# Gate products of a recurrent layer moved to VectorE, and another order of work in a spatial gating layer

## The chip, the cores and the metric

The kernel runs on one core of a Trainium2 chip. The metric is the device time of one execution in microseconds (us). The core has five engines that run their own instruction streams in order and meet at semaphores: TensorE (PE in the profile, its weight loads PEld), VectorE (DVE), ScalarE (ACT), GpSimd (POOL) and SyncE (SP, which issues the loads of the weights).

## What is computed

Two blocks on 512 tokens of width 1024. The first (a recurrent mixer, a sparse attention, a convolution and an MLP) is not touched. The second has a chunked spatial gating layer and a recurrent layer:

```python
def chunked_sgu_mixer(h, w_in, ln_w, ln_b, w_s, b_s, w_out):
    z = h @ w_in
    u, v, g = jnp.split(z, 3, axis=-1)                 # 2048 wide each
    u = jax.nn.gelu(u)
    v = layer_norm(jax.nn.gelu(v), ln_w, ln_b)
    s = jnp.einsum('gts,bnsgc->bntgc', w_causal, v) + b_s.T[None, None, :, :, None]
    y = u * s.reshape(B, S, A_WIDTH) * jax.nn.silu(g)
    return y @ w_out

def rglru_mixer(h, ...):
    xb, g = jnp.split(h @ w_in, 2, axis=-1)            # 1536 wide each, 12 heads of 128
    xc = conv_b + sum(conv_w[k] * shifted(xb, k))      # 4 taps
    r = sigmoid(gate_a(xc));  i = sigmoid(gate_x(xc))  # one 128x128 product per head
    a = exp(-RG_C * r * softplus(-lam))
    hseq = scan(a, sqrt(1 - a * a) * (i * xc))
    y = hseq * jax.nn.silu(g)
    return y @ w_out
```

## The kernel before

**Weights.** Every weight matrix is cut into units of 128 x 1024 numbers. A unit is loaded into one of 4 slots of `raw` (`RING = 4`), ScalarE writes its rounded part `w_hi` (`hi_unit`, L358), VectorE the rest `w_lo` (`lo_unit`, L370), three units ahead of their use (`LEAD = 3`). TensorE makes each product from three matmuls, hi by hi, hi by lo and lo by hi (`three`, L386 to L388); one unit is 24 matmuls of 512 columns. The order on every engine is written by hand, with counting semaphores; a Python `for` is unrolled, a `Fori` is a loop on the chip.

**Value rows (`v`).** Four groups `g`, each of four units (`v_unit`) and four blocks of 128 tokens `t`. When a group is done, ScalarE copies a block out of its bank (L1482, `vt`), squares it into one of two buffers `e0` (L1485), VectorE makes the argument of the tanh (L2075, L2077), ScalarE the tanh (L1487), VectorE the product (L2079) and the statistics (L2081, `v_stat`). Block `t` uses buffer `t % 2`. After the last group come the mean and variance, the root on ScalarE and its reciprocal on VectorE (L2084 to L2087).

**Gating loop.** Two halves of eight chunks, two chunks (`cc` 0 and 1) per turn of a `Fori`. A chunk is a `u` unit, a `g` unit and the spatial product `mix` (L1032), which reads the normalised values `vh` of that chunk. VectorE makes `vh` (L2095, four instructions, two buffers) at the head of the chunk, then two `lo_unit`, the gelu, the gate, and at the end `h_lo` (L2126); ScalarE makes squares, tanh, sigmoid and `h_hi`; GpSimd one product (L2335). Chunk `c` uses banks 4 to 6 or 0 to 2, so TensorE starts chunk `c` when `h_ready` says that VectorE has finished chunk `c - 2`. After eight chunks, `residual` multiplies their outputs by eight units of the output weights; its first unit takes the chunks in order, the last (`k = 7`) last.

**Recurrent loop.** Two heads per turn, six turns, the first unrolled. Per turn TensorE does units `project(0..3)` (banks 0, 1, 4, 5: `x` and `g` of the two heads) and `gates(0)`, `gates(1)` (L1056, L1057). ScalarE (`turn`, L1556 on) does: unit, `read_x(0)`, the decay curves of the turn before (exp, tanh, sqrt, with two table loads), two units, `read_x(1)`, `yb_high` for both heads (L1553), a table load, `read_gates(0)` (`t_r`, `t_i`), `read_g(0)` (`t_sg` the sigmoid, and `t_g` a copy of the bank), a unit, `read_gates(1)`, `read_g(1)`. GpSimd makes `t_i * xc` and `t_g * t_sg` (`gated`), then issues the loads of the next gate weights. VectorE (`turn`) does: `lo_unit`, `conv(0)`, `recurrence(0)` of the turn before, two `lo_unit`, `conv(1)`, `recurrence(1)`, two `yb_low`, `lo_unit`. The `g` banks are free when the copy `t_g` is made.

Of the kernel before, what the change touches and what calls it, by code (L numbers as in the profile page):

```python
# [156 lines left out]
def build(nc, a, out):  # L157
    with ExitStack() as ctx:
# [363 lines left out]
        def _(pe):  # L522
# [491 lines left out]
            for half in range(2):  # L1014
                pe.wait_ge(x_new, X_AO + KT * half)
                with pe.Fori(0, 4) as i:
                    for cc in range(2):
# [4 lines left out]
                        for s in range(2):
                            u = U_UG + 24 * half + 2 * cc + s
                            pe.wait_ge(split_lo, u + 1 + RING * i)
                            for k in range(KT):
                                last = three(pe, banks[:, 4 * (1 - cc) + s, :], unit(w_hi, u, P)[:, k, :],
                                             unit(w_lo, u, P)[:, k, :], n_hi[:, k, :], n_lo[:, k, :],
                                             k == 0, k == KT - 1)
                            last.then_inc(w_used, 1)
                        pe.wait_ge(vh_made, 8 * half + cc + 1 + 2 * i)  # L1030
                        for t in range(TT):
                            last = pe.matmul(banks[:, 4 * (1 - cc) + 2, t * P:(t + 1) * P], vh[:, cc, t, :],  # L1032
                                             wcT[:, bass.ds(i + 4 * half, 1), :].rearrange("p g t -> p (g t)"),
                                             start=True, stop=True)
                        last.then_inc(mixed, 1)
# [1351 lines left out]
```

## Time and profile before

| what | us |
|---|---|
| median of 3 runs | 1393.64 |
| lowest and highest of them | 1392.91, 1395.33 |
| the profiled execution's own time | 1392.23 |
| its span, from the first to the last instruction | 1390.0 |
| TensorE busy | 1279.1 (92%) |
| VectorE busy | 870.9 (63%) |
| ScalarE busy | 590.1 (42%) |
| GpSimd busy | 201.5 (14%) |

The span is 2.2 us shorter than its own execution's time, and that execution was 1.4 us faster than the median. The second block runs from about 755 us: value rows to 853, the gating loop and its output product to 1128, the recurrent layer to 1322, its output product to the end. A row of the timeline says when an instruction started, how long it took and, in brackets, how long its engine had been idle before it and what ended that. A row that comes back to back with the next one reads some 0.1 us longer than the distance of their starts.

### The profile page before, as it was taken

The page shows a single profiled execution, that of the slowest core. Times are in us where ns is not written, and L with a number is a line of the kernel's source. Part 1 is how long each engine was busy: PE and PEld are TensorE (multiplying, and loading weights), DVE is VectorE, ACT ScalarE, POOL GpSimd, SP SyncE. Part 2 cuts the span into 40 slices and gives each one's busy share as a digit, 9 for nine tenths or more (in the row PEclk, how much of TensorE's full clock was granted, in tenths as well). Part 3 has the DMA queues.
Part 4 walks back from the last instruction along what each step waited for, and adds up shares of the span by engine and source line. Part 5 has one row for each costly group of instructions (what it writes and reads, how often), then busy time and mean ns, then how long its engine had stood idle before and what let it go on. Part 6 is the DMA issues. An engine that isn't in the chain of part 4 may idle for free.

```text
span 1390.0 us, 18986 instructions
## 1 busy us (share of the span) xinstructions
PE 1279.1 (92%) x6581; PEld 1025.8 (74%) x6581; DVE 870.9 (63%) x1249; ACT 590.1 (42%) x834; POOL 201.5 (14%) x200
## 2 busy tenths in 40 slices
PE   6899478999899999999999998999999989989697
PEld 2678356778688788788888876888788867767476
DVE  4779988766765422344444886674466567767763
ACT  3475543551443211343333555442233336577542
POOL 6038864000000000000000000110011002233100
PEclk9999789999899999999999999999999999999899
DMA  8553212423545333233332222333222313223131
GB/s 304 152 178 87 61 47 62 122 76 121 153 138 151 105 98 98 82 100 92 100 96 76 76 82 84 89 93 103 79 81 86 106 54 100 81 68 91 34 102 61
DMA packets 204436, 137.87 MB, mean 99 GB/s; under 512 B 7074, under 2 KB 191569, under 8 KB 204384
## 3 DMA queue, kind: packets, MB, share of 16 engines
q1 hardware_dynamic: 200784, 134.40, 32.5%
q0 software_dynamic: 1376, 1.73, 0.4%
q10 hardware_dynamic: 2224, 1.05, 0.3%
q8 instruction: 32, 0.52, 0.2%
q14 instruction: 20, 0.16, 0.0%
HBM read 135.06 MB, written 2.10 MB: 99 GB/s over the span
## 4 chain that ended last, share of the span: by engine, by line
PE 62%; DVE 21%; ACT 7%; issue 7%; DMA 2%; DVEq 0%; ACTq 0%; SPq 0%
PE banks L386 19%; PE banks L387 19%; PE banks L388 19%; DVE w_lo L370 3%; ACT w_hi L358 2%; DVE xc L2168 1%; PE banks L1032 1%; DVE t_s L2188 1%; DMA raw<-in_ada_w 1%; DVE score L1731 1%; DVE score L1714 1%; DVE m L1728 1%; DVE vt L2079 1%; DVE e L2077 1%; ACT e L1487 1%
## 5 line engine op out<-in xcount | busy, mean ns | idle before, releaser
L370 DVE TENSOR_TENSOR w_lo<-raw,w_hi 128x1024 fp32r<-128x1024 f32 x204 | 264.1, 1302 | 175.2 <-ACT w_hi L358 172.6
L386 PE MATMUL banks<-h_hi,w_hi 128*128 128x512 f32 x824 | 332.6, 404 | 15.1 <-issue 4.7
L387 PE MATMUL banks<-h_lo,w_hi 128*128 128x512 f32 x824 | 324.6, 394 | 0.0
L388 PE MATMUL banks<-h_hi,w_lo 128*128 128x512 f32 x824 | 324.4, 394 | 0.0
L358 ACT ACTIVATE w_hi<-raw 128x1024 fp32r<-128x1024 f32 x204 | 213.0, 1052 | 166.2 <-PE banks L388 145.2
L386 PEld LDWEIGHTS banks<-h_hi,w_hi 128*128 128x128 f32 x824 | 157.4, 191 | 56.4 <-issue 13.4
L387 PEld LDWEIGHTS banks<-h_lo,w_hi 128*128 128x128 f32 x824 | 157.4, 191 | 33.9 <-issue 2.4
L388 PEld LDWEIGHTS banks<-h_hi,w_lo 128*128 128x128 f32 x824 | 157.0, 191 | 33.6
L386 PE MATMUL banks<-n_hi,w_hi 128*128 128x512 f32 x256 | 103.1, 403 | 1.2 <-DVE xT L1936 1.2
L386 PE MATMUL banks<-hid_hi,w_hi 128*128 128x512 f32 x256 | 102.7, 401 | 0.0
L387 PE MATMUL banks<-hid_lo,w_hi 128*128 128x512 f32 x256 | 102.4, 400 | 0.0
L388 PE MATMUL banks<-hid_hi,w_lo 128*128 128x512 f32 x256 | 102.2, 399 | 0.0
L387 PE MATMUL banks<-n_lo,w_hi 128*128 128x512 f32 x256 | 101.7, 397 | 0.0
L388 PE MATMUL banks<-n_hi,w_lo 128*128 128x512 f32 x256 | 101.7, 397 | 0.0
L2335 POOL TENSOR_TENSOR e<-e 128x512 f32<-128x512 f32 x16 | 20.7, 1291 | 410.0 <-DVE e L2112 410.0
L386 PE MATMUL banks<-w_hi,h_hi 128*128 128x512 f32 x160 | 64.5, 403 | 4.8 <-ACT hk L1212 2.6
L387 PE MATMUL banks<-w_lo,h_hi 128*128 128x512 f32 x160 | 63.0, 393 | 0.0
L388 PE MATMUL banks<-w_hi,h_lo 128*128 128x512 f32 x160 | 62.8, 393 | 0.0
L1409 ACT ACTIVATE sqb<-xT 128x512 f32 (+1 forms) x24 | 15.2, 632 | 110.9 <-DVE xT L1936 65.0
L1996 DVE TENSOR_TENSOR relu<-relu 128x512 f32<-128x512 f32 x32 | 22.1, 691 | 62.2 <-ACT relu L1445 62.2
L386 PEld LDWEIGHTS banks<-n_hi,w_hi 128*128 128x128 f32 x256 | 48.6, 190 | 12.6 <-issue 1.6
L388 PEld LDWEIGHTS banks<-hid_hi,w_lo 128*128 128x128 f32 x256 | 48.8, 191 | 11.9
(374 smaller groups left out, 1983.1 us busy)
## 6 DMA issues: line engine op xcount, KB each, us to landing
raw<-in_mlp_w SPq DMA_DIRECT2D x64, 512.0 KB, 4.0
raw<-in_a_w_in SPq DMA_DIRECT2D x48, 512.0 KB, 3.9
raw<-in_ada_w SPq DMA_DIRECT2D x40, 512.0 KB, 4.3
raw<-in_w_in SPq DMA_DIRECT2D x28, 512.0 KB, 3.8
raw<-in_b_w_in SPq DMA_DIRECT2D x24, 512.0 KB, 3.9
raw<-in_a_w_out SPq DMA_DIRECT2D x16, 512.0 KB, 3.7
raw<-in_b_w_out SPq DMA_DIRECT2D x16, 384.0 KB, 3.3
raw<-in_w_out SPq DMA_DIRECT2D x8, 512.0 KB, 4.4
```

The lines of the kernel that those rows point to most:

```text
L358: act.activation(dst, src, ACT.Copy).then_inc(split_hi, 1)
L370: dve.tensor_tensor(dst, src, hi, ALU.subtract).then_inc(split_lo, 1)
L386: pe.matmul(dst, l_hi, r_hi, start=first, stop=False)
L387: pe.matmul(dst, l_hi, r_lo, start=False, stop=False)
L388: return pe.matmul(dst, l_lo, r_hi, start=False, stop=last)
L1032: last = pe.matmul(banks[:, 4 * (1 - cc) + 2, t * P:(t + 1) * P], vh[:, cc, t, :], wcT[:, bass.ds(i + 4 * half, 1), :].rearrange("p g t -> ...
L1409: act.activation(sqb[:, t % 2, :], x, ACT.Square).then_inc(sq_made, 1)
L1487: act.activation(e0[:, t % 2, :], e0[:, t % 2, :], ACT.Tanh).then_inc(v_tanh, 1)
L1714: ins = dve.scalar_tensor_tensor(score[b][:, :], relus[:, i, 0:n], w, score[b][:, :], ALU.mult, ALU.add)
L1728: found[b] = chain.step(dve.max(m8[:, b - 1, :], score[b][:, :]))
L1996: dve.tensor_tensor(relu2[:, j % 2, :], relu[:, j % 2, :], relu[:, j % 2, :], ALU.mult)\
L2335: pool.tensor_tensor(e0[:, cc, :], e0[:, cc, :], e1[:, cc, :], ALU.mult).then_inc(ugp_made, 1)
```

## The change

**TensorE, gating.** The first turn of the first half is unrolled, and the `u` unit of chunk 1 stands ahead of the spatial product of chunk 0; the loop of that half then starts at turn 1. The second half's loop is as before.

**VectorE, gating.** `vh` of chunks 0 and 1 is made ahead of the loop; every chunk makes `vh` for the chunk two later at its end (the last two chunks make none).

**Value rows.** ScalarE and VectorE work on two token blocks in turns: on VectorE, L2075 and L2077 of block `t` stand ahead of L2079 and L2081 of block `t - 1`; on ScalarE, copy and square of block `t` stand ahead of the tanh of block `t - 1`.

**Recurrent layer.** GpSimd's `gated` is gone. VectorE multiplies `t_i` by `xc`, and `t_sg` by the `g` bank itself; ScalarE's copy `t_g` is gone. `gated(0)` stands behind the `yb_low` of VectorE's turn, `gated(1)` behind the unit that follows. TensorE waits for `gg_made` ahead of the `g` units, and GpSimd only loads gate weights. With two counts less, `evac` runs by 6 per turn instead of 8.

```diff
-                with pe.Fori(0, 4) as i:
+                def half_unit(cc, s, i):
+
+                    u = U_UG + 24 * half + 2 * cc + s
...
+                        last = three(pe, banks[:, 4 * (1 - cc) + s, :], unit(w_hi, u, P)[:, k, :],
...
+                    last.then_inc(w_used, 1)
+
+                def mix(cc, i):
+
+                    pe.wait_ge(vh_made, 8 * half + cc + 1 + 2 * i)
...
+                        last = pe.matmul(banks[:, 4 * (1 - cc) + 2, t * P:(t + 1) * P], vh[:, cc, t, :],
...
+                    last.then_inc(mixed, 1)
+
+                if half == 0:
+                    half_unit(0, 0, 0)
+                    half_unit(0, 1, 0)
+                    pe.wait_ge(evac, E_V + 13)
+                    half_unit(1, 0, 0)
+                    mix(0, 0)
+                    pe.wait_ge(evac, E_V + 16)
+                    half_unit(1, 1, 0)
+                    mix(1, 0)
+                with pe.Fori(1 - half, 4) as i:
                     for cc in range(2):
-
                         pe.wait_ge(h_ready, H_Y + 8 * half + cc - 1 + 2 * i)
-                        if cc == 1:
...
-                        for s in range(2):
...
+                        half_unit(cc, 0, i)
+                        half_unit(cc, 1, i)
+                        mix(cc, i)
...
-                pe.wait_ge(evac, E_RG + read - 8 + 8 * i)
+                if j % 2:
+                    pe.wait_ge(gg_made, (j + 1) // 2 - 2 + 2 * i)
+                else:
+                    pe.wait_ge(evac, E_RG + read - 6 + 6 * i)
...
+                pe.wait_ge(evac, E_RG + read - 6 + 6 * i)
...
-            project(3, 5, 8, 0)
...
-            gates(1, 8, 0)
+            gates(1, 6, 0)
...
                 project(0, 0, 1, i)
-                project(1, 1, 5, i)
+                project(1, 1, None, i)
...
-                project(3, 5, 8, i)
-                gates(1, 8, i)
-            pe.wait_ge(evac, E_RG + 4 * B_HEADS)
+                project(3, 5, None, i)
+                gates(1, 6, i)
+            pe.wait_ge(evac, E_RG + 3 * B_HEADS)
+            pe.wait_ge(gg_made, B_HEADS)
...
-                for t in range(TT):
+                for t in range(TT + 1):
                     n, bank = 4 * g + t, 4 * (1 - g % 2) + t
...
-                       .then_inc(v_copied, 1)
-                    act.wait_ge(v_stat, V0 + n - 1)
-                    act.activation(e0[:, t % 2, :], banks[:, bank, :], ACT.Square, scale=rs[:, t:t + 1]).then_inc(evac, 1)
-                    act.wait_ge(v_inner, n + 1)
-                    act.activation(e0[:, t % 2, :], e0[:, t % 2, :], ACT.Tanh).then_inc(v_tanh, 1)
...
+                        act.activation(vt[:, t, 512 * g:512 * (g + 1)], banks[:, bank, :], ACT.Copy, scale=rs[:, t:t + 1])\
...
+                        act.wait_ge(v_stat, V0 + n - 1)
+                        act.activation(e0[:, t % 2, :], banks[:, bank, :], ACT.Square, scale=rs[:, t:t + 1]).then_inc(evac, 1)
+                    if t:
+                        act.wait_ge(v_inner, n)
+                        act.activation(e0[:, (t - 1) % 2, :], e0[:, (t - 1) % 2, :], ACT.Tanh).then_inc(v_tanh, 1)
...
-                act.activation(t_g[:, cc, :], banks[:, 4 * cc + 1, :], ACT.Copy).then_inc(evac, 1)
...
-                for t in range(TT):
...
-                    dve.tensor_scalar(e, e, GELU_C * GELU_A, GELU_C, ALU.mult, ALU.add).then_inc(v_aff, 1)
...
-                    dve.tensor_tensor(e, e, v, ALU.mult).then_inc(v_inner, 1)
-                    dve.wait_ge(v_tanh, n + 1)
-                    dve.scalar_tensor_tensor(v, e, 1.0, v, ALU.add, ALU.mult).then_inc(v_gelu, 1)
...
-                    dve.bn_stats(vst[:, t, g, :], v).then_inc(v_stat, 1)
+                for t in range(TT + 1):
+                    if t < TT:
...
+                        dve.tensor_tensor(e, e, v, ALU.mult).then_inc(v_inner, 1)
+                    if t:
+                        n = 4 * g + t - 1
...
+                        dve.wait_ge(v_tanh, n + 1)
+                        dve.scalar_tensor_tensor(v, e, 1.0, v, ALU.add, ALU.mult).then_inc(v_gelu, 1)
...
+                        dve.bn_stats(vst[:, t - 1, g, :], v).then_inc(v_stat, 1)
...
+            def values(cc, c, i):
...
+                for t in range(TT):
+                    ins = dve.tensor_scalar(vh[:, cc, t, :], vt[:, t, bass.ds(i * 2 * P + c * P, P)],
...
+                ins.then_inc(vh_made, 1)
+
+            values(0, 0, 0)
+            values(1, 1, 0)
             for half in range(2):
-                with dve.Fori(0, 4) as i:
+
+                def chunk(cc, i, ahead):
+
...
+                    dve.wait_ge(h_ready, H_Y + c - 1 + 2 * i)
+                    lo_unit(dve, u + LEAD, i)
...
+                    lo_unit(dve, u + 1 + LEAD, i)
...
+                    if ahead:
+                        values(cc, c + 2, i)
+
+                with dve.Fori(0, 4 - half) as i:
...
+                        chunk(cc, i, True)
+                if half == 1:
+                    for cc in range(2):
+                        chunk(cc, 3, False)
...
+            def gated(cc, i):
+
+                dve.wait_ge(evac, E_RG + (4, 6)[cc] + 6 * i)
+                dve.tensor_tensor(t_i[:, cc, :], t_i[:, cc, :], xc[:, cc, :], ALU.mult).then_inc(ix_made, 1)
+                dve.wait_ge(g_sig, 2 * KT + cc + 1 + 2 * i)
+                dve.tensor_tensor(t_g[:, cc, :], t_sg[:, cc, :], banks[:, 4 * cc + 1, :], ALU.mult).then_inc(gg_made, 1)
+
...
+                gated(0, i)
                 lo_unit(dve, U_B + 3 + LEAD, i)
+                gated(1, i)
...
-            def gated(i):
-                for cc in range(2):
-                    pool.wait_ge(evac, E_RG + (4, 7)[cc] + 8 * i)
-                    pool.tensor_tensor(t_i[:, cc, :], t_i[:, cc, :], xc[:, cc, :], ALU.mult).then_inc(ix_made, 1)
-                    pool.wait_ge(evac, E_RG + (5, 8)[cc] + 8 * i)
-                    pool.tensor_tensor(t_g[:, cc, :], t_g[:, cc, :], t_sg[:, cc, :], ALU.mult).then_inc(gg_made, 1)
-
...
-                gated(i)
...
-            gated(B_HEADS // 2 - 1)
```

VectorE, value rows, from the first block of the third group (`e<-e 128x512` is L2075, `vt<-e,vt` the product with the tanh). Before:

```order
L2075 TENSOR_SCALAR e<-e 128x512
L2077 TENSOR_TENSOR e<-e,vt 128x512
L2079 SCALAR_TENSOR_TENSOR vt<-e,vt 128x512
L2081 BN_STATS vst<-vt 128x6
L2075 TENSOR_SCALAR e<-e 128x512
L2077 TENSOR_TENSOR e<-e,vt 128x512
L2079 SCALAR_TENSOR_TENSOR vt<-e,vt 128x512
L2081 BN_STATS vst<-vt 128x6
```

and now (lines 2099, 2101, 2106 and 2108 are the same four):

```order
L2099 TENSOR_SCALAR e<-e 128x512
L2101 TENSOR_TENSOR e<-e,vt 128x512
L2099 TENSOR_SCALAR e<-e 128x512
L2101 TENSOR_TENSOR e<-e,vt 128x512
L2106 SCALAR_TENSOR_TENSOR vt<-e,vt 128x512
L2108 BN_STATS vst<-vt 128x6
L2099 TENSOR_SCALAR e<-e 128x512
L2101 TENSOR_TENSOR e<-e,vt 128x512
L2106 SCALAR_TENSOR_TENSOR vt<-e,vt 128x512
L2108 BN_STATS vst<-vt 128x6
```

Two blocks' arguments now stand ahead of the first product with a tanh.

VectorE, from the last statistics of the value rows into the gating loop. Before:

```order
L2081 BN_STATS vst<-vt 128x6
L2084 BN_AGGR vmv<-vst 128x2 x4
L2087 RECIPROCAL vrs<-vrs 128x4
L2089 UNCONDITIONAL_BRANCH
L2089 ISA
L2095 ISA
L2095 TENSOR_SCALAR vh<-vt,vmv,vrs 128x128
```

and now:

```order
L2108 BN_STATS vst<-vt 128x6
L2111 BN_AGGR vmv<-vst 128x2 x4
L2114 RECIPROCAL vrs<-vrs 128x4
L2118 TENSOR_SCALAR vh<-vt,vmv,vrs 128x128 x8
L2165 UNCONDITIONAL_BRANCH
L2165 ISA
L363 ISA
L370 TENSOR_TENSOR w_lo<-raw,w_hi 128x1024
L2133 REGISTER_ALU
L2134 TENSOR_SCALAR e<-e 128x512
```

Eight `vh` instructions stand ahead of the loop, and the loop's first work is a unit.

ScalarE, the unrolled first turn of the recurrent layer. Before:

```order
L1523 ACTIVATE t_r<-banks,par 128x512
L1526 ACTIVATE t_i<-banks,par 128x512
L1531 ACTIVATE t_sg<-banks 128x512
L1532 ACTIVATE t_g<-banks 128x512
L358 ACTIVATE w_hi<-raw 128x1024
L1523 ACTIVATE t_r<-banks,par 128x512
L1526 ACTIVATE t_i<-banks,par 128x512
L1531 ACTIVATE t_sg<-banks 128x512
L1532 ACTIVATE t_g<-banks 128x512
```

and now:

```order
L1547 ACTIVATE t_r<-banks,par 128x512
L1550 ACTIVATE t_i<-banks,par 128x512
L1555 ACTIVATE t_sg<-banks 128x512
L358 ACTIVATE w_hi<-raw 128x1024
L1547 ACTIVATE t_r<-banks,par 128x512
L1550 ACTIVATE t_i<-banks,par 128x512
L1555 ACTIVATE t_sg<-banks 128x512
```

The two copies into `t_g` are gone, so each unit `w_hi` follows the sigmoid `t_sg`.

VectorE, the end of a turn of the recurrent loop, from the two `yb_lo`. Before:

```order
L2195 REGISTER_ALU
L2197 ISA
L2197 TENSOR_TENSOR yb_lo<-t_b,yb_hi 128x512
L2195 REGISTER_ALU
L2197 ISA
L2197 TENSOR_TENSOR yb_lo<-t_b,yb_hi 128x512
L363 REGISTER_ALU
L370 TENSOR_TENSOR w_lo<-raw,w_hi 128x1024
L2217 REGISTER_ALU
L2217 COMPARE_AND_BRANCH
```

and now, behind the same two `yb_lo`:

```order
L2238 REGISTER_ALU
L2239 TENSOR_TENSOR t_i<-t_i,xc 128x512
L2240 REGISTER_ALU
L2241 TENSOR_TENSOR t_g<-t_sg,banks 128x512
L363 REGISTER_ALU
L370 TENSOR_TENSOR w_lo<-raw,w_hi 128x1024
L2238 REGISTER_ALU
L2239 TENSOR_TENSOR t_i<-t_i,xc 128x512
L2240 REGISTER_ALU
L2241 TENSOR_TENSOR t_g<-t_sg,banks 128x512
L2268 REGISTER_ALU
L2268 COMPARE_AND_BRANCH
```

Four products were put around the last unit of the turn.

## Rows read from the trace of the kernel before

**Rows 1.** The head of the profile page

```profile
span 1390.0 us, 18986 instructions
```

**Rows 2.** Waits of TensorE, 756 to 1330 us: who waited, for whom: total, times, longest

```profile
PE banks L386 <- ACT t_g L1532: 14.0, 4, 9.9
PE banks L1032 <- DVE vh L2095: 5.7, 1, 5.7
PE banks L1056 <- DVE xc L2168: 3.4, 5, 0.9
...
PE banks L386 <- DVE w_lo L370: 2.2, 2, 1.2
PE banks L386 <- DVE yb_lo L2197: 1.8, 1, 1.8
```

**Rows 3.** TensorE, timeline: start, us, line, what, [idle before and what ended it]

```profile
855.32 0.63 PE L388 MATMUL banks<-n_hi,w_lo 128*128 128x512 f32 x1
...
866.88 1.05 PE L1032 MATMUL banks<-wcT,vh 128*128 x8
...
939.44 1.05 PE L1032 MATMUL banks<-wcT,vh 128*128 x8
...
945.11 0.39 PE L386 MATMUL banks<-h_hi,w_hi 128*128 128x512 f32 x1
```

**Rows 4.** VectorE, timeline, last group of value rows

```profile
836.99 0.43 DVE L2075 TENSOR_SCALAR e<-e 128x512 f32<-128x512 f32 x1 [3.73 <-ACT e L1485]
...
838.85 0.69 DVE L2079 SCALAR_TENSOR_TENSOR vt<-e,vt 128x512 f32<-128x512 f32 x1 [0.70 <-ACT e L1487]
...
849.09 0.69 DVE L2081 BATCH_NORM_STATS2 vst<-vt 128x6 f32<-128x512 f32 x1
```

**Rows 5.** ScalarE, timeline, same place

```profile
839.29 0.68 ACT L1485 ACTIVATE e<-banks,rs 128x512 f32<-128x512 f32 x1
```

**Rows 6.** VectorE, timeline, first loop of the gating stage

```profile
851.32 1.12 DVE L2095 TENSOR_SCALAR vh<-vt,vmv,vrs 128x128 f32 x4 [0.34 <-DVE vrs L2087]
853.18 1.23 DVE L370 TENSOR_TENSOR w_lo<-raw,w_hi 128x1024 fp32r<-128x1024 f32 x1 [0.74 <-ACT w_hi L358]
...
862.86 0.69 DVE L2126 TENSOR_TENSOR h_lo<-e,h_hi 128x512 f32 x1 [0.93 <-ACT h_hi L1506]
...
940.26 0.69 DVE L2112 TENSOR_TENSOR e<-e,banks 128x512 f32<-128x512 f32 x1 [0.83 <-ACT e L1503]
...
944.11 0.69 DVE L2126 TENSOR_TENSOR h_lo<-e,h_hi 128x512 f32 x1 [0.92 <-ACT h_hi L1506]
```

**Rows 7.** TensorE, timeline, loop of the recurrent layer

```profile
1177.66 1.02 PE L1056 MATMUL banks<-xc,gw 128*128 128x512 f32 x2
...
1202.96 1.02 PE L1056 MATMUL banks<-xc,gw 128*128 128x512 f32 x2
...
1247.52 0.50 PE L386 MATMUL banks<-h_hi,w_hi 128*128 128x512 f32 x1 [1.34 <-ACT t_g L1532]
```

**Rows 8.** ScalarE, timeline, the same loop

```profile
1186.98 0.63 ACT L1553 ACTIVATE yb_hi<-t_b 128x512 f32 x1 [8.00 <-DVE t_b L2192]
...
1243.28 0.63 ACT L1553 ACTIVATE yb_hi<-t_b 128x512 f32 x1 [9.30 <-DVE t_b L2192]
...
1246.86 0.61 ACT L1532 ACTIVATE t_g<-banks 128x512 f32<-128x512 f32 x1
1247.34 1.08 ACT L358 ACTIVATE w_hi<-raw 128x1024 fp32r<-128x1024 f32 x1
...
1299.55 0.63 ACT L1553 ACTIVATE yb_hi<-t_b 128x512 f32 x1 [9.30 <-DVE t_b L2192]
```

**Rows 9.** VectorE, timeline, first product of a turn of that loop

```profile
1251.52 2.14 DVE L370 TENSOR_TENSOR w_lo<-raw,w_hi 128x1024 fp32r<-128x1024 f32 x1 [1.35 <-ACT w_hi L358]
```

**Rows 10.** TensorE, timeline, a wait in the first block

```profile
144.53 0.50 PE L386 MATMUL banks<-w_hi,h_hi 128*128 128x512 f32 x1 [2.64 <-ACT hk L1212]
```

More of the change, by code:

```diff
@@ L1015, in _ @@
                 pe.wait_ge(x_new, X_AO + KT * half)
-                with pe.Fori(0, 4) as i:
+                def half_unit(cc, s, i):
+                    u = U_UG + 24 * half + 2 * cc + s
+                    pe.wait_ge(split_lo, u + 1 + RING * i)
+                    for k in range(KT):
+                        last = three(pe, banks[:, 4 * (1 - cc) + s, :], unit(w_hi, u, P)[:, k, :],
+                                     unit(w_lo, u, P)[:, k, :], n_hi[:, k, :], n_lo[:, k, :],
+                                     k == 0, k == KT - 1)
+                    last.then_inc(w_used, 1)
@@ new lines, in mix @@
+                def mix(cc, i):
+                    pe.wait_ge(vh_made, 8 * half + cc + 1 + 2 * i)
+                    for t in range(TT):
+                        last = pe.matmul(banks[:, 4 * (1 - cc) + 2, t * P:(t + 1) * P], vh[:, cc, t, :],
+                                         wcT[:, bass.ds(i + 4 * half, 1), :].rearrange("p g t -> p (g t)"),
+                                         start=True, stop=True)
+                    last.then_inc(mixed, 1)
[8 more added lines that the diff above has]
+                    mix(1, 0)
@@ L1017, in _ @@
+                with pe.Fori(1 - half, 4) as i:
                     for cc in range(2):
                         pe.wait_ge(h_ready, H_Y + 8 * half + cc - 1 + 2 * i)
-                        if cc == 1:
-                            pe.wait_ge(evac, E_V + 16)
-                        for s in range(2):
[L1023 to L1029, printed above, removed]
@@ L1030, in _ @@
-                        pe.wait_ge(vh_made, 8 * half + cc + 1 + 2 * i)
-                        for t in range(TT):
[L1032 to L1035, printed above, removed]
+                        half_unit(cc, 0, i)
@@ L1053, in gates @@
                 pe.wait_ge(gw_in[cc], 32 + 32 * i)
-                pe.wait_ge(evac, E_RG + read - 8 + 8 * i)
+                pe.wait_ge(evac, E_RG + read - 6 + 6 * i)
                 pe.wait_ge(xc_made, cc + 1 + 2 * i)
@@ L1060, in _ @@
             first_units(U_B, (0, 1, 4), H_RG, h_hi, h_lo)
-            project(3, 5, 8, 0)
+            pe.wait_ge(split_lo, U_B + 4)
+            for k in range(KT):
+                last = three(pe, banks[:, 5, :], unit(w_hi, U_B + 3, P)[:, k, :], unit(w_lo, U_B + 3, P)[:, k, :],
+                             h_hi[:, k, :], h_lo[:, k, :], k == 0, k == KT - 1)
+            last.then_inc(w_used, 1)
             gates(0, 4, 0)
-            gates(1, 8, 0)
+            gates(1, 6, 0)
             with pe.Fori(1, B_HEADS // 2) as i:
                 project(0, 0, 1, i)
-                project(1, 1, 5, i)
+                project(1, 1, None, i)
                 project(2, 4, 2, i)
                 gates(0, 4, i)
-                project(3, 5, 8, i)
-                gates(1, 8, i)
-            pe.wait_ge(evac, E_RG + 4 * B_HEADS)
+                project(3, 5, None, i)
+                gates(1, 6, i)
+            pe.wait_ge(evac, E_RG + 3 * B_HEADS)
+            pe.wait_ge(gg_made, B_HEADS)
             pe.wait_ge(h_ready, H_YB + B_HEADS - 2)
@@ L2154, in conv @@
             def conv(cc, i, first=False):
-                dve.wait_ge(evac, E_RG + cc + 1 + 8 * i)
+                dve.wait_ge(evac, E_RG + cc + 1 + 6 * i)
                 if not first:
```

89 lines of the change are left out of this document (43 added, 46 removed).

## The prediction

> **What bounds the kernel now.** I read the page's head for the span, then who waits for whom on TensorE in the second block, then the timelines around each of those waits. TensorE is busy 92% of the span, so only its waits, and what it does at a low clock, can be won. In the stages that the change touches it waits 2.2 us in two pieces for `w_lo` (value rows), 5.7 us once for `vh` (start of the gating loop), 14.0 us in four pieces for `t_g`, 3.4 us in five pieces for `xc` and 1.8 us for the last `yb_lo` [rows 2]. Of the 14.0, one piece of 9.9 us is at the end of the recurrent loop. So the reader should see two places: around 853 us, and the loop from 1158 to 1322 us. What matters is which chain decides each place, since TensorE's idle time comes back only as far as the chain behind it shortens.
>
> **Value rows in turns.** Before, VectorE waits 0.70 us in each block for the tanh [rows 4]; one group takes 849.09 + 0.69 - 836.99 = 12.8 us from its first argument to its last statistics [rows 4]. With two blocks in turns the first two blocks run without a wait. But there are two buffers `e0`, and ScalarE may square block 2 only when the statistics of block 0 are made, which is VectorE's instruction just before the argument of block 2. So blocks 2 and 3 wait for a square, 0.68 us [rows 5] plus some 0.05 at either end, 0.75 in all; the tanh is hidden then. The gain is 4 x 0.70 - 2 x 0.75 = 1.3 us per group, not 2.8. Where it counts: in the groups ahead of the last, VectorE reaches its next units 1.3 us earlier, and both waits for `w_lo` (the longer is 1.2) [rows 2] go: 2.2 us. In the last group the work starts when TensorE has finished its last unit, so there the 1.3 us come on top.
>
> **The third unit and `vh` ahead.** After the last value row unit TensorE has two units to do and then waits 5.7 us. With a third unit of some 5.6 us (two units and a spatial product take (939.44 - 866.88) / 6 = 12.1 us [rows 3]) this wait is covered, and with it the matmuls at 0.63 instead of 0.40 us that follow it, at the 1.2 GHz level of the clock [rows 3]. Taken alone TensorE would stand at its next gate, chunk 2, some 10 us earlier: 2.2, 5.7, and about 2.3 for the slow spatial product and 7 slow matmuls. But chunk 2 needs VectorE's end of chunk 0, and from there VectorE's chain decides. From `h_lo` of chunk 0 to `h_lo` of chunk 7 it takes 944.11 - 862.86 = 81.2 us [rows 6], TensorE 72.6 us for the six chunks between [rows 3]. In this chain VectorE waits for TensorE only once, 0.83 us for the last sigmoid [rows 6]; the rest is its own work and its exchange with ScalarE and GpSimd, which the change leaves. So the gain at the end of the half is the gain at chunk 0 plus 0.8. At chunk 0: 2.2 + 1.3 from above, less 0.3, since the second `vh` (about 1.03 of the 1.12 us, back to back) stands where VectorE idled 0.74 us for `w_hi` [rows 6]. That is 3.2, with the 0.8 then 4.0 us at `h_lo` of chunk 7, which ended at 944.80 and now ends at 940.8. TensorE's first matmul with `k = 7` started at 945.11 [rows 3], 0.3 after that, without a wait; now it waits for it and starts at about 940.85. **Gain 4.3 us.** TensorE should show new waits of some 2 to 3 us at chunk 2 and again at `k = 7`. A wait of 2.64 us in the first block was followed by matmuls of 0.50 and then no slow ones on the trace [rows 10], the 5.7 us wait by slow ones [rows 2, 3]; I take no clock loss, and keep 1.5 us for it (7 matmuls some 0.2 us longer). In the second half nothing is won: there the loop starts behind the residual sums and TensorE sets the pace. The unrolled turn issues no DMA and passes none; SyncE's loads hang on `w_lo`, which comes earlier.
>
> **The recurrent loop.** The turn is 28.14 us: from ScalarE's second `yb_hi` of one turn to the next, (1299.55 - 1186.98) / 4 [rows 8]. TensorE alone would do it in 25.3 us, as in the turn from 1177.66 to 1202.96, which had no wait in it [rows 7]. The loop that decides runs through ScalarE (table load, gates of head 0, copy, unit, gates of head 1, copy, unit) to VectorE's first `lo_unit` of the next turn, and on through its convolutions and recurrences to `yb_hi` again. In it:
> - Two copies `t_g` go: each takes 1247.34 - 1246.86 = 0.48 us of ScalarE [rows 8], 0.96 per turn.
> - VectorE's `lo_unit` there takes 2.14 us [rows 9], elsewhere 1.23 [rows 6]. It is the one under which GpSimd's last gate product lies. With GpSimd's products gone I take 1.23, so 0.91 more. If the length came from ScalarE's writing or from a transfer it would stay; bounds 0 and 0.91, and I take 0.91 as it is the same instruction of the same shape. The Trainium skill (SBUF — State Buffer, Who interferes with whom) says that a VectorE instruction with two SBUF inputs contends with a GpSimd instruction that reads SBUF; by that rule the 0.91 goes too.
> - Four products come, 0.69 us each by the products with a bank or with SBUF operands on VectorE [rows 4, 6], about 0.61 back to back, 2.4 per turn. They stand where VectorE idles for `w_hi`: 1.35 us ahead of that `lo_unit` [rows 9] and more ahead of the unit before. Counted from `yb_hi` at 1243.28: the copy started at 3.6, there `w_hi` starts now and ends at 4.7 [rows 8]. `gated(0)` then runs from 3.2 to 4.5, the unit from 4.7 to 5.8, `gated(1)` from 5.9 to 7.1, and the next `w_hi` is ready at 8.2 - 0.96 = 7.2 (the `lo_unit` of 1251.52 [rows 9] followed it). So they are hidden, but `gated(1)` by 0.1 us only; if the cover is missed, each product costs 0.6. Bounds 0 and 1.2 per turn (the two of `gated(1)`); I take 0.
> - The wait of `project(1)` for the `g` bank now ends with VectorE's product, at 4.5 us instead of 4.2 (1247.52 less 1243.28 [rows 7, 8]). Behind it stand only TensorE's own units, and TensorE has 26.3 - 25.3 = 1.0 us of slack per turn, so it costs nothing.
> - GpSimd's weight loads are issued earlier, right after `gates_made`; they have a turn to land.
>
> So 28.14 becomes 28.14 - 0.96 - 0.91 = 26.27, above TensorE's 25.3. Four such turns: 4 x 1.87 = 7.5 us. The first turn gains nothing, as its decay curves wait for TensorE. In the tail ScalarE's decay curves come 0.96 us earlier for the two copies, so the last `yb_lo` does; TensorE waits 1.8 us for it [rows 2], which covers the 0.96. **Gain 7.5 + 1.0 = 8.5 us**; I take 8.4 for a small new loss at the products.
>
> **Sum.** 4.3 + 8.4 = 12.7 us. The span of 1390.0 [rows 1] becomes 1377.3, its execution 1392.23 - 12.7 = 1379.5, and the median 1393.64 - 12.7 = 1380.9. Less than half of the idle time listed at the start comes back.
>
> **Rivals**, each as a median:
> - *Half-measure A, the slow `lo_unit` stays*: 4 x 0.91 = 3.6 less, 1384.6. For it: ScalarE and transfers are active there too. 0.12.
> - *B, the change doesn't do what it says*: two `e0` buffers make the value rows as serial as before. Then 3.5 us of chunk 0's gain go, 1384.4. Against it: the first two blocks need no freed buffer. 0.08.
> - *C, the products aren't covered*: 1.2 per turn, 4.9 in all, 1385.8. 0.07.
> - *D, TensorE decides in the gating half*: if VectorE's chain behind chunk 0 shortens too, what chunk 2 gains stays. It started at 866.88 + 0.8 = 867.7 [rows 3] and would start with `h_lo` of chunk 0, at 863.55 - 3.2 = 860.4 [rows 6], so 7.3 instead of 4.3; 1377.9. Against it: the chain had only one wait for TensorE. 0.08.
> - *E, slower*: VectorE becomes the bound of the recurrent loop. Its place is the turn; it decides once a turn is longer than 28.14 + 4.3 / 4 = 29.2 us, and by over 0.2% from 29.9. If the four products were wholly on the path at 1.3 us (twice VectorE's 0.69, if operands in a bank or a port slow them), a turn would be 28.14 + 5.2 - 1.9 = 31.4 and the median 1393.6 - 4.3 + 4 x 3.3, with the tail about 1403. The Trainium skill (Perfetto Trace Analysis, Optimizing Scalar/DVE Operations) advises offloading to ScalarE or GpSimd where VectorE is saturated, which speaks against this move. In the trace VectorE idles ahead of both units, so 0.04.
>
> **Numbers.** The forecast, 1380.9 (own range 1378.5 to 1383.0), 0.58; A to E as above, together 0.39; nothing measurable 0.03. The range of 8 in 10 takes in A, B, C and D: 1376.5 to 1386.5. The measurement of this kernel tells some 0.2% (2.8 us) from no change. Faster by over 0.2%: 0.93 (the forecast and A to D); within 0.2%: 0.03; slower: 0.04.
>
> **What would show it.** Right if: no `w_lo` waits from 800 to 835 us; the group of value rows takes 11.4 us with waits for a square, not a tanh; no wait at the spatial product, but one of 2 to 3 us at chunk 2 and at `k = 7`; `yb_hi` every 26.3 us; the first `lo_unit` of a turn at 1.23 us; `gated(1)` just ahead of `w_hi`; the last wait for `yb_lo` at 0.9. Wrong if the turn stays above 27 us, or if the half's output product starts its `k = 7` at another distance than 4 us, or if a stretch at 1.2 GHz appears behind the new waits.

## The result and the profile after

| | before | after |
|---|---|---|
| median, us | 1394.49 (6 runs) | 1387.66 (6 runs) |
| lowest and highest | 1391.88, 1396.76 | 1384.71, 1389.24 |
| the profiled execution's own time | 1392.23 | 1385.49 |
| its span | 1390.0 | 1383.9 |

The ratio is 0.9945, 95% interval 0.9929 to 0.9961: faster by 7.7 us (5.4 to 9.9). The sign was right, but the gain is 0.6 of the 12.7 us forecast, and the median lies 1.2 us above the range. The six runs of before have their median 0.85 us above that of the three runs that the forecast was counted from.

The head of the page of after:

```profile
span 1383.9 us, 18935 instructions
## 1 busy us (share of the span) xinstructions
PE 1279.5 (92%) x6581; PEld 1026.9 (74%) x6581; DVE 877.8 (63%) x1273; ACT 584.0 (42%) x822; POOL 169.1 (12%) x176
```

VectorE took over 24 products, ScalarE lost 12 copies, GpSimd 24 products. TensorE's busy time grew by 0.4 us though its work is the same: somewhere it ran at a lower clock.

Waits of TensorE in after, 750 to 1330 us (who waited, for whom: total, times, longest):

```profile
PE banks L386 <- DVE t_g L2241: 13.9, 4, 9.6
PE banks L386 <- DVE h_lo L2159: 5.0, 2, 2.7
...
PE banks L1073 <- DVE xc L2210: 0.3, 1, 0.3
PE banks L386 <- DVE yb_lo L2246: 0.3, 1, 0.3
```

Against [rows 2], the waits for `w_lo` (2.2) and `vh` (5.7) are gone and those for `xc` are 0.3 instead of 3.4. Two waits for `h_lo` are new, 5.0 us together. The waits for `t_g` add up to 13.9 us where they were 14.0.

Where the time went, as starts on TensorE in the two profiled executions:

| place | before | after | difference |
|---|---|---|---|
| first matmul of the second block's value stage | 754.30 | 755.25 | +0.95 |
| `k = 7` of the first half's output product | 945.11 | 940.75 | -4.36 |
| second half | 985.21 | 982.61 | -2.60 |
| first unit of the recurrent layer | 1134.10 | 1132.10 | -2.00 |
| its first gates | 1157.33 | 1155.98 | -1.35 |
| its output product | 1306.85 | 1301.31 | -5.54 |
| the second part of that product | 1322.06 | 1315.65 | -6.41 |
| last statistics | 1380.58 | 1374.16 | -6.42 |

The 0.95 us at the start comes out of the first block, which the change leaves alone. From there to `k = 7` 5.3 us are won; then 1.76 are given back in one product; 0.6 and 0.65 go in stretches with the same instructions; the recurrent loop wins 4.2 and its tail 0.9. The 0.6 are small matmuls at the end of the gating layer that run slower (two groups of eight, 1.46 and 2.08 us instead of 1.05 and 1.88), and the 0.65 are eight matmuls of 0.63 us instead of five behind a wait of 2.27 us. Across all eleven traces that last number is 5 to 11, so it is not a mark of the change.

**Value rows and chunk 0.** VectorE of after, the last group of value rows and what follows (start, us, line, what, [idle before and what ended it]):

```profile
835.18 0.43 DVE L2099 TENSOR_SCALAR e<-e 128x512 f32<-128x512 f32 x1 [4.16 <-ACT e L1508]
...
839.57 0.43 DVE L2099 TENSOR_SCALAR e<-e 128x512 f32<-128x512 f32 x1 [0.75 <-ACT e L1508]
...
842.81 0.43 DVE L2099 TENSOR_SCALAR e<-e 128x512 f32<-128x512 f32 x1 [0.76 <-ACT e L1508]
...
845.91 0.70 DVE L2108 BATCH_NORM_STATS2 vst<-vt 128x6 f32<-128x512 f32 x1
...
850.02 1.23 DVE L370 TENSOR_TENSOR w_lo<-raw,w_hi 128x1024 fp32r<-128x1024 f32 x1
...
859.68 0.69 DVE L2159 TENSOR_TENSOR h_lo<-e,h_hi 128x512 f32 x1 [0.92 <-ACT h_hi L1530]
```

The group takes 845.91 + 0.70 - 835.18 = 11.4 us instead of 12.8 [rows 4], with two waits for a square and none for a tanh. `h_lo` of chunk 0 starts 3.2 us before that of [rows 6].

**The half's end.** TensorE of after, at chunk 2 and at `k = 7`:

```profile
860.51 0.49 PE L386 MATMUL banks<-n_hi,w_hi 128*128 128x512 f32 x1 [2.40 <-DVE h_lo L2159]
...
940.75 0.50 PE L386 MATMUL banks<-h_hi,w_hi 128*128 128x512 f32 x1 [2.65 <-DVE h_lo L2159]
...
942.18 0.63 PE L388 MATMUL banks<-h_hi,w_lo 128*128 128x512 f32 x1
...
944.75 0.63 PE L388 MATMUL banks<-h_hi,w_lo 128*128 128x512 f32 x1
945.17 0.44 PE L386 MATMUL banks<-h_hi,w_hi 128*128 128x512 f32 x1
```

From some 1.4 us behind the second wait on, matmuls come every 0.43 us instead of every 0.23, at the 1.2 GHz level of the clock: from 942.2 to 945.1 us the granted clock is 0.50. A view by stretches, up to the start of the second half, gives its mean (the 0.96 and 1.00 behind the five engines' busy times), after first, then before:

```profile
940.70:982.60 41.90, 40.68 (x171) 33.16 (x171) 16.10 (x21) 8.59 (x9) 0.00 (x0) 0.96 0.34 100
```

```profile
945.10:985.20 40.10, 38.94 (x172) 31.92 (x170) 15.40 (x18) 8.49 (x8) 0.00 (x0) 1.00 0.37 105
```

The same product takes 1.8 us longer.

**The recurrent loop.** ScalarE of after, second `yb_hi` of the first and of the last of five turns, and the root between:

```profile
1185.59 0.64 ACT L1576 ACTIVATE yb_hi<-t_b 128x512 f32 x1 [8.00 <-DVE t_b L2234]
...
1251.47 1.28 ACT L1571 ACT_TABLE_LOAD   x1
1252.77 1.15 ACT L1571 ACTIVATE t_s<-t_r 128x512 f32<-128x512 f32 x2
...
1294.09 0.63 ACT L1576 ACTIVATE yb_hi<-t_b 128x512 f32 x1 [9.30 <-DVE t_b L2234]
```

The turn is (1294.09 - 1185.59) / 4 = 27.12 us: before 28.14, forecast 26.27. VectorE of after in one of these turns:

```profile
1246.30 0.68 DVE L2241 TENSOR_TENSOR t_g<-t_sg,banks 128x512 f32<-128x512 f32 x1
1247.12 1.23 DVE L370 TENSOR_TENSOR w_lo<-raw,w_hi 128x1024 fp32r<-128x1024 f32 x1
...
1253.51 0.69 DVE L2224 SCALAR_TENSOR_TENSOR t_s<-t_a,t_s 128x512 f32<-128x512 f32 x1 [0.91 <-ACT t_s L1571]
```

The unit takes 1.23 us instead of 2.14 [rows 9], as forecast, and the products are done just ahead of it. But the 0.91 us won there come back to the hundredth as a wait for ScalarE's root.

### The profile page after: what moved, and what is told of

The parts are those of the page before. It is cut to its first block, busy times and chain, and to the rows that moved or that the text cites. A ratio compares the mean times of both kernels' runs of the same rounds, so it can differ in the third digit from the quotient of the medians.

```text
span 1383.9 us, 18935 instructions
## 1 busy us (share of the span) xinstructions
PE 1279.5 (92%) x6581; PEld 1026.9 (74%) x6581; DVE 877.8 (63%) x1273; ACT 584.0 (42%) x822; POOL 169.1 (12%) x176
## 3 DMA queue, kind: packets, MB, share of 16 engines
q10 hardware_dynamic: 2224, 1.05, 0.3%
## 4 chain that ended last, share of the span: by engine, by line
PE 64%; DVE 18%; ACT 8%; issue 7%; DMA 2%; POOL 1%; DVEq 0%; ACTq 0%; SPq 0%; POOLq 0%
PE banks L386 20%; PE banks L387 19%; PE banks L388 19%; DVE w_lo L370 3%; ACT w_hi L358 2%; DMA raw<-in_ada_w 1%; DVE score L1754 1%; DVE score L1737 1%; DVE m L1751 1%; DVE t_s L2230 1%; DVE xc L2210 1%; DVE hq L1788 1%; POOL e L2386 1%; DVE hgt L1715 1%; DVE hk L1791 1%
## 5 line engine op out<-in xcount | busy, mean ns | idle before, releaser
L370 DVE TENSOR_TENSOR w_lo<-raw,w_hi 128x1024 fp32r<-128x1024 f32 x204 | 256.4, 1264 | 146.2 <-ACT w_hi L358 142.1
```

What stands on the lines that cost most here:

```text
L370: dve.tensor_tensor(dst, src, hi, ALU.subtract).then_inc(split_lo, 1)
```

## Experiments

Gains are against the kernel before in runs of the same chip: 1 less the ratio, times the median of before, with the 95% interval of the ratio. x1 to x4 went together, x5 to x7, x8 and x9, so a comparison across these groups goes by gains. There are eleven traces in all: before, after and x1 to x9.

### x1 and x2: the two halves of the change

x1 has the value rows and the gating loop of after, and the recurrent layer of before:

```diff
+                for t in range(TT + 1):
...
+                    half_unit(1, 0, 0)
+                    mix(0, 0)
...
+            values(0, 0, 0)
+            values(1, 1, 0)
```

> Only the value rows in turns, vh ahead and the third unit; the recurrent layer is that of before. Theory: the gain at the first matmul with k = 7 is 4.3 us as forecast (5.3 on the changed kernel once its later start of the stage is taken off), and 1.8 us of it go again, since the wait of 2.65 us there is followed by matmuls at 1.2 GHz. So about 3 us faster than before, 1391 for 1394, and on the trace 7 or 8 slow matmuls (0.63 us each) behind the wait at k = 7. Rival 1: the slow matmuls there are chance, they are missing here, and the kernel is 4.5 to 5 us faster. Rival 2: the front part gives nothing at all, and the whole gain of 6.8 us is that of the recurrent layer: within 1 us of before.

x2 has only the recurrent layer of after:

```diff
-                act.activation(t_g[:, cc, :], banks[:, 4 * cc + 1, :], ACT.Copy).then_inc(evac, 1)
...
+                gated(0, i)
                 lo_unit(dve, U_B + 3 + LEAD, i)
+                gated(1, i)
```

> Only the recurrent layer's change; value rows and gating loop are those of before. Theory: a turn (second yb_hi to second yb_hi) takes 27.1 us instead of 28.14, since the relieved lo_unit is swallowed by a wait of 0.9 us for ScalarE's square root; four turns give 4.1 us and the tail 0.9, together 5 us, so 1389.5 for 1394.5. Rival (the forecast's size, 26.3 us per turn with the loss elsewhere in the changed kernel, as from the shifted start): 8.4 us, 1386.

x1: 1390.58 us (12 runs), ratio 0.9973 (0.9962 to 0.9985), 3.8 us. x2: 1390.82 us (10 runs), ratio 0.9973 (0.9962 to 0.9984), 3.8 us. Expected were 3 and 5 us. Together they make 7.6 against 7.7 for the whole change, which fits halves that do not disturb each other, but it is no sharp test: the medians alone lie 5.0 and 4.8 us below before, 9.8 together against 6.8. The recurrent half clearly gave less than its term of 8.4; the interval of the front half, 2.1 to 5.3 us, still takes in its 4.3. TensorE of x1:

```profile
940.36 0.50 PE L386 MATMUL banks<-h_hi,w_hi 128*128 128x512 f32 x1 [2.65 <-DVE h_lo L2152]
...
941.58 0.63 PE L387 MATMUL banks<-h_lo,w_hi 128*128 128x512 f32 x1
```

ScalarE of x2:

```profile
1187.68 0.63 ACT L1560 ACTIVATE yb_hi<-t_b 128x512 f32 x1 [8.00 <-DVE t_b L2199]
...
1296.19 0.63 ACT L1560 ACTIVATE yb_hi<-t_b 128x512 f32 x1 [9.30 <-DVE t_b L2199]
```

The slow stretch at `k = 7` belongs to the front half, the turn of (1296.19 - 1187.68) / 4 = 27.13 us to the recurrent half.

### x3: `k = 7` later

In the first half's output product, TensorE does `k = 0` to 6 of the first two units before `k = 7` of either; for this the first four units are unrolled. All else is as in after.

```diff
+                    for j in range(2):
+                        pe.wait_ge(split_lo, U_UG + 16 + j + 1)
+                        first_sums(j, 0, KT - 1)
+                    for j in range(2):
+                        first_sums(j, KT - 1, KT).then_inc(w_used, 1)
```

> The changed kernel with one more edit: in the output product of the first half, TensorE takes k = 0 to 6 of the first two units before k = 7 of both. Theory: at TensorE's arrival VectorE is 2.65 us short of h_lo of chunk 7; with 4.8 us of other matmuls in between there is no wait and no stretch at 1.2 GHz behind it: 2.65 + 1.8 = 4.4 us faster than the changed kernel, about 1383.3, ratio to before 0.992. Rival (the two halves are coupled elsewhere, so the wait moves to the next gate, the sums ahead of the second half, or the clock falls there instead): as fast as the changed kernel, 1387.7.

1383.0 us (5 runs), ratio 0.9913 (0.9900 to 0.9926), 12.1 us. TensorE of x3 waits for another engine once, at chunk 2, and from there to the second half the granted clock is 1.00:

```profile
861.96 0.49 PE L386 MATMUL banks<-n_hi,w_hi 128*128 128x512 f32 x1 [2.40 <-DVE h_lo L2180]
```

```profile
861.90:980.00 118.10, 116.63 (x528) 95.36 (x528) 71.97 (x119) 45.69 (x57) 9.04 (x7) 1.00 0.34 98
```

From chunk 2 to the second half it is 118.1 us, against 982.61 - 860.51 = 122.1 in after. With the wait of 2.65 us the slow stretch went too.

### x4 and x7: without the square root

ScalarE's root in the decay curves becomes a copy, so one table load per turn goes and the curves end earlier. The kernels leave out the square root; all other work is done. x4 is made from after, x7 from before.

```diff
-                    act.activation(t_s[:, cc, :], t_r[:, cc, :], ACT.Sqrt)
+                    act.activation(t_s[:, cc, :], t_r[:, cc, :], ACT.Copy)
```

> The changed kernel, but ScalarE copies instead of taking the square root of the decay (t_s), which leaves out one table load of 1.28 us ahead of it, in every turn; the value of the recurrence's input factor is left out with it. Theory: the wait of 0.9 us ahead of VectorE's t_s product goes and the turn is 26.2 to 26.3 us, as the forecast had it from VectorE's side. Rival (the turn is held at 27.1 by something else, TensorE's order or VectorE's own work): the wait goes, or moves, and the turn stays at 27.1.

> The kernel before, with the square root of the decay left out in the same way (a copy, without the table load). Theory: in the kernel before VectorE came to its t_s product just as the square root was ready, the turn was held by VectorE and ScalarE's gate reads, so the turn stays 28.1 us. Rival (the square root's chain held the turn before too): the turn falls by about 0.9 us or more.

ScalarE and, last, VectorE of x4:

```profile
1211.01 0.63 ACT L1576 ACTIVATE yb_hi<-t_b 128x512 f32 x1 [8.50 <-DVE t_b L2234]
...
1289.72 0.63 ACT L1576 ACTIVATE yb_hi<-t_b 128x512 f32 x1 [9.27 <-DVE t_b L2234]
```

```profile
1250.02 0.69 DVE L2224 SCALAR_TENSOR_TENSOR t_s<-t_a,t_s 128x512 f32<-128x512 f32 x1
```

ScalarE of x7:

```profile
1217.72 0.63 ACT L1553 ACTIVATE yb_hi<-t_b 128x512 f32 x1 [9.30 <-DVE t_b L2192]
...
1302.14 0.63 ACT L1553 ACTIVATE yb_hi<-t_b 128x512 f32 x1 [9.30 <-DVE t_b L2192]
```

x4: a turn of (1289.72 - 1211.01) / 3 = 26.24 us, against 26.27 in the forecast, no wait for the root, 1380.34 us in its one run. x7: (1302.14 - 1217.72) / 3 = 28.14 us, what it was with the root, 1393.81 us in its one run (before: 1395.71). So ScalarE's decay curves did not hold the turn before, and do after. The turns come from the traces; one run is too little to read a gain from.

### x5 and x6: value rows alone, third unit alone

x5 is before with the value rows of two blocks in turns, nothing else:

```diff
-                for t in range(TT):
+                for t in range(TT + 1):
...
+                    if t:
+                        act.wait_ge(v_inner, n)
```

> Only the value rows in turns (ScalarE and VectorE), everything else of before. Theory: both waits for w_lo go (2.2 us and some 0.5 for two restarts) and each group of value rows is 1.3 us shorter; TensorE waits 4.4 us for vh instead of 5.7, is 4.1 us ahead at chunk 2 and keeps that, since VectorE's chain and TensorE move together: 4 us faster than before, 1390.5. Rival: the waits for w_lo come back elsewhere (units, raw slots), under 1.5 us.

x6 is before with the unrolled first turn on TensorE and `vh` made ahead on VectorE, the value rows as they were:

```diff
+                    pe.wait_ge(evac, E_V + 13)
+                    half_unit(1, 0, 0)
+                    mix(0, 0)
...
+                    if ahead:
+                        values(cc, c + 2, i)
```

> Only vh ahead of the loop and the third unit, value rows of before. Theory: the 5.7 us wait goes from its place, but h_lo of chunk 7 comes only 0.5 us earlier (0.8 for the sigmoid less 0.3 for the second vh), so TensorE waits some 3 us at chunk 2 and again at k = 7, and a stretch at 1.2 GHz behind the latter costs about 1.8: between 0 and 1.5 us slower than before, 1395. Rival (TensorE's 5.7 us wait and its slow clock are what holds the stage): 5 to 7 us faster.

x5: 1392.02 us (9 runs), ratio 0.9972 (0.9961 to 0.9983), 3.9 us. x6: 1394.86 us (12 runs), ratio 0.9992 (0.9982 to 1.0002), 1.1 us and not told from none. TensorE of x5:

```profile
851.92 1.88 PE L1032 MATMUL banks<-wcT,vh 128*128 x8 [4.40 <-DVE vh L2101]
```

TensorE of x6:

```profile
855.93 0.48 PE L386 MATMUL banks<-n_hi,w_hi 128*128 128x512 f32 x1 [1.20 <-DVE w_lo L370]
...
865.06 0.49 PE L386 MATMUL banks<-n_hi,w_hi 128*128 128x512 f32 x1 [2.40 <-DVE h_lo L2146]
...
945.36 0.79 PE L386 MATMUL banks<-h_hi,w_hi 128*128 128x512 f32 x1 [2.71 <-DVE h_lo L2146]
```

In x5 TensorE still waits 4.4 us for `vh`, and the kernel gains as much as x1, which has both parts. x6 was expected at 0 to 1.5 us slower than before; its interval, 0.3 slower to 2.5 us faster, leaves that open. In its trace the `vh` wait of 5.7 us became three others (1.20 + 2.40 + 2.71 = 6.3 us) and the slow stretch moved to `k = 7`. Most of TensorE's idle time had only changed its place.

### x8 and x9: does the third unit pay with `k = 7` late?

x8 is x3 without the third unit: gating loop and `vh` of before. x9 is the kernel of x3 again, beside it. From x8's edit against x3:

```diff
-                    half_unit(1, 0, 0)
-                    mix(0, 0)
...
-            values(0, 0, 0)
-            values(1, 1, 0)
```

> The kernel of x3 without the third unit ahead: the gating loop and vh as before the change, but value rows in turns, the new recurrent loop, and k = 7 of the first two units behind k = 0 to 6 of both. Theory: the late k = 7 pays only where TensorE comes to it early, and it comes early only by what the third unit gives it. In x5 (no third unit) TensorE waited 4.4 us for vh and then not once up to k = 7, so there is nothing for the late k = 7 to win: x8 gives what value rows and recurrent loop give, 3.9 + 3.8 = 7.7 us, a median near 1387 (ratio 0.9945), 4 to 5 us above x3. In its trace: a vh wait of 4.4 us near 852 with slow matmuls behind it, no wait at chunk 2 and none at k = 7, turns of 27.1 us. Rival: the late k = 7 is worth its 4.6 us by itself (less idle time of TensorE at the half's end, whatever stands ahead), then x8 lies with x3, ratio 0.9913, and the third unit gives nothing in any kernel.

> The kernel of x3 once more, beside x8 on the same chip, as the reference point for it. Theory: ratio 0.9913 within 0.0015, no wait and no slow matmuls at k = 7, a wait of 2.4 us at chunk 2 with none behind it. If the gain of x3 was the luck of one chip or of short slow stretches, the ratio comes out at 0.993 or more.

x8: 1386.2 us (6 runs), ratio 0.9934 (0.9919 to 0.9948), 9.2 us. x9: 1382.33 us (6 runs), ratio 0.9908 (0.9893 to 0.9924), 12.8 us. TensorE of x8, then of x9:

```profile
851.34 2.07 PE L1032 MATMUL banks<-wcT,vh 128*128 x8 [4.40 <-DVE vh L2129]
```

```profile
859.60 0.50 PE L386 MATMUL banks<-n_hi,w_hi 128*128 128x512 f32 x1 [2.40 <-DVE h_lo L2180]
```

The medians are 3.9 us apart. The third unit is worth that if `k = 7` is late, and the late `k = 7` does little without it: x8 is 1.5 us better than the whole change, inside both intervals. x8 gained more than the 7.7 us expected, also inside its interval.

The traces separate the parts more sharply than the medians do. From the first matmul of the second block to the start of the second half TensorE takes:

| value rows in turns | third unit | `k = 7` late | traces | us |
|---|---|---|---|---|
| no | no | no | before, x2, x7 | 230.9, 230.2, 231.6 |
| yes | no | no | x5 | 226.3 |
| no | yes | no | x6 | 231.5 |
| yes | yes | no | after, x1, x4 | 227.4, 227.4, 227.3 |
| yes | no | yes | x8 | 226.8 |
| yes | yes | yes | x3, x9 | 223.3, 223.3 |

The first row shows how far traces with the same parts can differ: 1.4 us, as the slow matmuls behind the `vh` wait vary. The value rows are worth 4.6 us. Neither the third unit alone nor the late `k = 7` alone makes this stretch shorter (x6, x8; after and x1 against x5), both together make it 3.0 us shorter: each pays only with the other. x3 and x9 agree, so this kernel lies 12 to 13 us below before and 4 to 5 below after.

## Why the prediction was wrong

**Value rows: right.** A group of 11.4 us, two waits for a square of 0.75, no `w_lo` wait. x5 gives 3.9 us where 2.2 + 1.3 = 3.5 were counted.

**Third unit and `vh` ahead: right as a chain, and next to nothing as a gain.** TensorE waits 2.40 us at chunk 2 and 2.65 at `k = 7` ("2 to 3 us"), which starts at 940.75 (forecast 940.85). That the start agrees is luck: this execution entered the stage 0.95 us late, so 5.3 us were won where 4.3 were counted. Of the 1.0 more, 0.6 us was there when the last value unit ended (2.77 net for 2.2); what made it is open. The third unit added nothing to it: the gains of x1 and x5 (3.8 and 3.9 us, each give or take some 1.5) can't tell 0.8 us, but up to the second half x5's trace is 1.1 us shorter than those of after and x1 (226.3 and 227.4 us), so the 0.8 us that the forecast gave to it did not reach the second half.

**The clock: the first mis-sized term, 1.8 us.** The prediction took no clock loss behind the new waits, "and keep 1.5 us for it". The loss came in all four kernels with the early `k = 7` and the third unit (after, x1, x4, x6), 6 to 8 slow matmuls each, and 1.8 us in after. The step that failed was to rest this on one row, the wait of 2.64 us without slow matmuls [rows 10]. That row could not carry it: only six matmuls stand behind the wait, and the last is followed by 17 us of idle time.

```profile
145.80 0.39 PE L388 MATMUL banks<-w_hi,h_lo 128*128 128x512 f32 x1
163.52 1.94 PE L693 MATMUL banks<-hq,hk 128*32 128x32 f32 x128 [17.33 <-DVE hf L1745]
```

The six are over 1.7 us behind the first one's start, and at `k = 7` of after the first matmul of 0.63 us starts 1.4 us behind it. So the row would have shown a stretch that begins at once, as in x6, but hardly one like that of after. In this same place of the first block, a wait of 2.61 to 2.66 us is followed by slow matmuls in five of the eleven traces, x2 being one:

```profile
146.36 0.79 PE L386 MATMUL banks<-w_hi,h_hi 128*128 128x512 f32 x1 [2.61 <-ACT hk L1220]
146.95 0.63 PE L387 MATMUL banks<-w_lo,h_hi 128*128 128x512 f32 x1
```

And the trace of before had rows against it, which I had not drawn on:

```profile
466.53 2.25 PE L538 MATMUL banks<-ones,acc 128*128 128x1 f32 x16 [2.61 <-DVE acc L2002]
468.64 0.77 PE L386 MATMUL banks<-hid_hi,w_hi 128*128 128x512 f32 x1
469.22 0.63 PE L387 MATMUL banks<-hid_lo,w_hi 128*128 128x512 f32 x1
...
1134.10 0.77 PE L386 MATMUL banks<-h_hi,w_hi 128*128 128x512 f32 x1 [2.27 <-issue]
1134.67 0.63 PE L387 MATMUL banks<-h_lo,w_hi 128*128 128x512 f32 x1
```

The first is the nearest: a wait of 2.61 us with no other in the 85 us before it, with 13 matmuls of 0.63 us behind it here and 5 or 6 in each of the other ten traces. What differs from `k = 7` is that sixteen small matmuls (one column each, 2.25 us) come between. The second, and one like it at 374.24 (2.43 us), stand some 6 us behind another wait. None is alike in all, but each was nearer to the question than one row with a kind answer.

**Copies: right.** 0.96 us per turn. The turn became 28.14 - 27.12 = 1.02 shorter. No run takes out the copies alone; that the 0.96 of the 1.02 are theirs is an estimate from their length.

**`lo_unit` relieved: right in size, wrong in its place. This is the missed step.** The instruction went from 2.14 to 1.23 us, in every turn. That GpSimd's products had made it long is supported by after's 1.23 us under ScalarE's work with GpSimd idle, and by all eleven traces: from the second turn on it takes 2.13 to 2.18 us in the five whose kernels have these products on GpSimd and 1.22 to 1.23 in the six others (the unit before it 1.72 to 1.76 and 1.22 to 1.23). The Trainium skill (SBUF — State Buffer, Who interferes with whom) has this contention as a rule, and the trace agrees with it. But I had let "the loop that decides" run through VectorE's `lo_unit` alone, and added 0.96 and 0.91. The loop forks behind the second `w_hi`: one arm is `lo_unit`, the convolution and the first two steps of the recurrence on VectorE, the other `read_x`, table load, exp, tanh, table load and root on ScalarE. They meet at the product `t_s`. In before, ScalarE, then VectorE:

```profile
1257.17 1.15 ACT L1548 ACTIVATE t_s<-t_r 128x512 f32<-128x512 f32 x2
```

```profile
1257.95 0.69 DVE L2182 SCALAR_TENSOR_TENSOR t_s<-t_a,t_s 128x512 f32<-128x512 f32 x1
```

VectorE starts without a wait, but the first of the two roots had ended only about 0.2 us before (1257.17 + 1.15 / 2 = 1257.75). In after, where it does wait, it starts 0.16 us behind that end (1253.51 against 1252.77 + 0.58), so the slack of the other arm was some 0.04 us. The copies stood ahead of the fork and shortened both arms; the relief stood in one of them. What was left of it is 1.02 - 0.96 = 0.06 us per turn: 0.85 us lost, 4 x 0.85 = 3.4 us in all. x4 and x7 show it from both sides: with the root gone after runs at 26.24, and before does not change.

**Products: right.** They are hidden; `gated(1)` ends just ahead of the unit. TensorE's waits at the `g` unit (1.52 us instead of 1.34 [rows 7]) cost nothing.

**Tail: right in its gain, not in the wait that was to show it.** It won 0.9 us for the 1.0 counted, but the last `yb_lo` wait is 0.3 and not 0.9. TensorE of after:

```profile
1301.31 0.77 PE L386 MATMUL banks<-yb_hi,w_hi 128*128 128x512 f32 x1 [9.65 <-DVE t_g L2241]
...
1315.65 0.50 PE L386 MATMUL banks<-yb_hi,w_hi 128*128 128x512 f32 x1 [0.29 <-DVE yb_lo L2246]
```

Behind its long wait there were 12 slow matmuls instead of 8, which filled the rest. x2 had 5 and a `yb_lo` wait of 1.63 us, and its second part starts at the same distance, 14.33 us (after 14.34): slow matmuls ahead of a wait cost nothing here.

**The sum.** 12.7 - 3.4 (the other arm) - 1.8 (clock) = 7.5 us, against 7.7 (5.4 to 9.9) by the ratio and 6.8 between the medians. In the profiled execution, 5.3 + 4.2 + 0.9 - 1.76 - 0.6 - 0.65 - 0.95 = 6.4 us. Of the last three, 0.6 and 0.65 are TensorE's low clock lasting longer at places that the change leaves alone, and 0.95 comes out of the first block; none is shown to come from the change. So the close 7.5 is partly luck: 1.0 us more was won early, and 2.2 us were lost where nothing was counted.

**The rivals.** None was what happened. B (value rows as serial as before) is ruled out by the group of 11.4 us, whose first two blocks run without a wait. A (the slow `lo_unit` stays, 1384.6) and C (products not covered, 1385.8) had a loss per turn of the size seen, 0.91 and 1.2 for 0.85, by other mechanisms; their own signs (a unit of 2.14, a product behind `w_hi`) are absent. E's turn of 31.4 us did not come: the four products take 0.68 to 0.69 us each, with an operand in a bank too, and stand where VectorE had been idle. D's 7.3 us did not come in after, since VectorE's chain decided; x3 and x9, which put `k = 7` where that chain no longer stops TensorE, bring it in (in x9 the second half starts at 977.65 instead of 985.21, 7.6 us earlier, with the second block's start at 754.34). Each loss had been weighed alone, but both together give 1380.9 + 3.4 + 1.8 = 1386.1 us, still just inside the range. What put the median outside is the rest: 0.85 us because the six runs of before lie higher than the three that were counted from, and 0.7 us that the medians don't resolve.

## What to carry to other kernels

Before adding two savings on a loop, walk back from each join and ask when the other input was ready: an arm that is no more than a tenth of a us early caps whatever is saved on this side, and the view of waits shows nothing of it, as nobody waits yet. Filling a wait with later work pays only if the consumer that stops TensorE next moves too; here the third unit gave nothing until `k = 7` was moved behind other sums, and 3.9 us then (3.5 in the traces). And a new wait of some us on TensorE should be priced with the slow matmuls behind it, from all rows of that kind and not from one; a row counts as free of them only if enough work stands behind the wait to show them.

## What the runs showed of the hardware

- The same wait of 2.61 to 2.66 us, at one place in an unchanged first block, was followed by slow matmuls in five traces and by none in six, with only six matmuls behind it to tell by. At another place of that block a wait of 2.61 was followed by them in all eleven. At `k = 7` waits of 2.63 to 2.71 were followed by them four times in four; at chunk 2 waits of 2.40 never in six.
- Where a slow stretch begins also varies: with the first matmul behind the wait (0.79 us in x6), or 0.8 us (x1) to 1.1 us (after) later, counted to the first matmul that takes longer (0.61 and 0.59 us).
- VectorE's `lo_unit` took 2.13 to 2.18 us with GpSimd's products beside it and 1.22 to 1.23 without.
- The matmuls of 0.63 us in a trace number 62 to 89 across the eleven traces (70 before, 80 after), each some 0.2 us longer. The difference of 27 is 5 us, nearly the gain in question: the whole times of single executions can't tell parts of this change apart, and medians of some ten runs barely can. The distance between two places in a trace does better, where the slow matmuls between them are counted along.
